# Product of the q and k weights in the middle of projection 1, on projection 2's weight buffer, with ScalarE forming the weights' high parts

## The chip, the cores and the metric

One core of one Trainium2 chip. The metric is the device time of the whole kernel in microseconds (us), lower is better; kernels are compared by the median of their runs. The engines are TensorE (PE, with its weight loads as PEld), VectorE (DVE), ScalarE (ACT), GpSimd (POOL) and SP, which only issues DMAs here.

## The reference

A decoder layer on 1024 tokens of width 1024 in float32. With h the modulated norm of the input:

```
proj = h @ w_in                      # xa, va, oa, za, gates, qa, ka, vat, zb, ga, gb
xc   = silu(causal_conv(xa))         # per channel, width 4
q_m  = xc_head @ w_q[head];  k_m = xc_head @ w_k[head] / 16
h_m  = mlstm_chunkwise(q_m, k_m, v_m, i, f)       # 4 heads of 256
o_a  = merged dilated window attention            # 3 groups x 4 heads of 128
y    = sigmoid(ga) * (h_m' @ w_out_mlstm) + sigmoid(gb) * (o_a' @ w_out_attn)
out  = rms_norm(x + gate * (y @ w_out))
```

What matters here is `w_in`, which is multiplied chunk by chunk, and that the kernel never forms q_m and k_m both: scores are xc (w_q w_k^T) xc^T, so each head multiplies its q weights with its k weights once (256x256 from 256 terms).

## The kernel before

Every float32 product with weights is done in three passes (`three_pass`, L477): each operand is split into a high part, the value rounded to the matmul's input type, and a low part, the rest; high x high, high x low and low x high are added up in the bank.

The stages are setup, mixing (`mix`, L484), merging (`merge`, L1174), finishing. The mixing stage runs over 4 heads. For each head there are 19 weight chunks of 128x1024, numbered q in the order of use: 18 projections (n = 0 to 17) and one chunk with the q and k weights of the head, at place FOLD = 3 (L37). Projections 0 and 1 make the inputs of the convolution; 2 to 5 are projections over tokens (values and output gate; matmuls of 256 columns, `project_tokens`, L612), the others (`project`, L598) have matmuls of 512. Each is done in two halves of the tokens, h = 0 and 1, of 24 matmuls of 512 or 48 of 256.

The path of a chunk: SP loads it into `wraw[q % 2]` (`load`, L528) once the split of chunk q - 2 is done. GpSimd splits it (`gpsimd`, L578): the high part into `whi[q % 2]`, as an addition of zero, and then the low part into `wlo[q % 2]`. It starts when chunk q - 2 has been multiplied (the semaphore `proj`, which every half counts up by one, and the weight product by two) and when the load has landed. TensorE waits for `w_split`, which the low part counts up. So while TensorE works on one buffer, the other is loaded with parts.

TensorE runs its program in order (`tensor`, L592). In its loop over n (L748) `fold_weights` (L638) stands ahead of projection 3: 12 matmuls of 256 columns into bank A1. Between the halves of projection 5 it uses this product (`head_q`); from projection 6 on the mLSTM's chunks, and from 9 on attention, lie between the halves.

ScalarE (`scalar`, L775) copies each half's bank out (`keep`), which frees the bank for the same half of the next projection (semaphores `kept`). Behind `keep` of either half come its other duties: sigmoids of the convolution, splitting xc and the weight product (`xc_high`, `fold_high`), exponentials. In projection 17 it first waits (L911) for the softmax statistics of all groups: they go out to DRAM by SP (`save_stats`), come back by another layout (`turn_stats`, which stands behind the load issued in projection 17), and VectorE works on them (`weigh_groups`, L1087) before ScalarE's exponential. Only then ScalarE copies out the second half of projection 17.

VectorE runs the convolution beside projections 0 and 1, then `fold_low` and `merge_groups` of the head before. In head 0 it first ends the setup: a chain of operations on the 4x1024 gate rows (L433 to L447), whose results SP writes to DRAM (L265 to L267), waits for, and reads back (L560, L561) before its first load of the stage, which is projection 3's weights (L564). The weights of the first four chunks were loaded in the setup.

Of the kernel before, what the change touches and what calls it, by code (L numbers as in the profile page):

```python
# [20 lines left out]
P = 128  # L21
D = 1024
S = 1024
KT = D // P
# [9 lines left out]
KSCALE = DH ** -0.5  # L34
MAIN = 18
CHUNKS = MAIN + 1
FOLD = 3  # L37
MERGE0 = HEADS * CHUNKS

XA, VA, OA, QKV, ZA, ZB = 0, 2, 4, 6, 15, 17  # L40
# [1 line left out]
AHEAD = 4  # L42
NADA = 5
PI = float(np.pi)


class Steps:
# [20 lines left out]
def stored(ap, g, lo=0, n=S):  # L68

    d = DIL[g]  # L70
    return ap.rearrange("p (r u) -> p r u", r=d)[:, :, lo // d:(lo + n) // d]


def build(nc, a, out):
# [409 lines left out]
def mix(nc, a, sem, ps, T):  # L484
# [12 lines left out]
    cb = [qm[:, 0, :], qm[:, 1, :], vt[:].rearrange("p c q -> p (c q)")]  # L497
    tn = [turn[:, b, 3:3 + S] for b in range(2)]

    summed, o_sig = sem("summed"), sem("o_sig")  # L500
    fold_split = sem("fold_split")
    xc_high_done, xc_split, zb_done = sem("xc_high_done"), sem("xc_split"), T["zb_done"]
    hp_in, ready, gr_in, hc_turned, hc_done = (T["hp_in"], *(sem(n) for n in ("mix_ready", "gr_in", "hc_turned", "hc_done")))
# [73 lines left out]

    def gpsimd(pool):  # L578
        pool.sem_inc(w_split, 2)
        for q in range(MERGE0):  # L580
            raw, hi, lo = wraw[:, q % 2, :], whi[:, q % 2, :], wlo[:, q % 2, :]
            pool.wait_ge(proj, 2 * q + 2)
            pool.wait_ge(w_in[q % 2], (q // 2 + 1) * 16)
            nc.gpsimd.tensor_tensor(hi, raw, zero[:].broadcast_to([P, D]), ALU.add).then_inc(pool_s, 1)  # L584
            pool.wait_ge(pool_s, q + 1)
            nc.gpsimd.tensor_tensor(lo, raw, hi.bitcast(F32), ALU.subtract).then_inc(w_split, 1)  # L586

    def blocks(g, tile):
# [3 lines left out]
    def tensor(pe):  # L592
        t_ = nc.tensor
        for i in range(0, HEADS):
# [3 lines left out]
            def project(n, h):  # L598
                q = chunk(n)
                pe.wait_ge(w_split, q + 3)  # L600
                pe.wait_ge(kept[h], i * MAIN + n + 1)
                for k in range(KT):
                    mm = three_pass(t_, ps[:, h, :], whi[:, q % 2, k * P:(k + 1) * P], wlo[:, q % 2, k * P:(k + 1) * P],
                                    h_hi[:, k, h * HALF:(h + 1) * HALF], h_lo[:, k, h * HALF:(h + 1) * HALF],
                                    k == 0, k == KT - 1)
                mm.then_inc(proj, 1)
# [5 lines left out]
            def project_tokens(n, h):  # L612

                q = chunk(n)
                pe.wait_ge(w_split, q + 3)
                if n == VA and h == 0:
                    pe.wait_ge(out_used, i * 4 + 4)
                    pe.wait_ge(masked, i * 24 + 1)
                if n == OA and h == 0:
                    pe.wait_ge(kept[0], i * MAIN + XA + 3)  # L620
                    pe.wait_ge(kept[1], i * MAIN + XA + 3)
                if n == OA and h == 1:
                    pe.wait_ge(p_kept, i * 12 + 1)
                    pe.wait_ge(pv_kept, i * 12 + 1)
                    pe.wait_ge(hc_done, 2)
                    pe.wait_ge(fold_split, i * 2 + 2)
                if n in (VA + 1, OA + 1):
                    pe.wait_ge(kept[h], i * MAIN + n + 1)
                for c in range(4 * h, 4 * h + 4):
                    to = ps[:, TOKEN_BANKS[n // 2 * 2][c // 2], (c % 2) * DH:(c % 2 + 1) * DH]  # L630
                    for j in range(KT // 2):
                        k = n % 2 * (KT // 2) + j
                        w = slice(j * DH, (j + 1) * DH)
                        mm = three_pass(t_, to, h_hi[:, k, c * P:(c + 1) * P], h_lo[:, k, c * P:(c + 1) * P],
                                        whi[:, q % 2, w], wlo[:, q % 2, w], j == 0, j == KT // 2 - 1)
                mm.then_inc(proj, 1)

            def fold_weights():  # L638

                q = i * CHUNKS + FOLD  # L640
                pe.wait_ge(w_split, q + 3)
                pe.wait_ge(p_kept, i * 12 + 1)
                pe.wait_ge(pv_kept, i * 12 + 1)
                w_hi, w_lo = (w[:, q % 2, :].rearrange("p (j e d) -> p j e d", j=2, e=2) for w in (whi, wlo))
                for d in range(2):
                    for e in range(2):
                        cols = slice(d * P, (d + 1) * P)
                        mm = three_pass(t_, A1[:, d * DH:(d + 1) * DH], w_hi[:, 0, e, cols], w_lo[:, 0, e, cols],
                                        w_hi[:, 1, e, :], w_lo[:, 1, e, :], e == 0, e == 1)
                mm.then_inc(proj, 2)  # L650
# [96 lines left out]

            for n in range(MAIN):  # L748
                c, g = n - 7, (n - 9) // 3
                if n == FOLD:  # L750
                    fold_weights()
                product = project_tokens if VA <= n < QKV else project
                product(n, 0)
                if n == 5:
                    head_q()
                if n == 6:
                    scores_and_keys(0)
                if 0 <= c < NCH:
                    numerator(c)
                if n >= 9:  # L760
                    attend(g, 2 * (n - 9 - 3 * g))
                product(n, 1)
                if n == 2 and i == 0:
                    pe.wait_ge(gr_in, 16)
                    pe.wait_ge(pv_kept, 1)
                    t_.transpose(A2[:, 0:P], gr[:], ident[:]).then_inc(hc_turned, 1)
                if 0 <= c < NCH - 1:
                    state_update(c)
                    scores_and_keys(c + 1)
                if n == 15:  # L770
                    turn_output()
                if n >= 9:
                    attend(g, 2 * (n - 9 - 3 * g) + 1)

    def scalar(act):  # L775
# [2 lines left out]
        act.sem_inc(pv_kept, 1)  # L778

        for i in range(0, HEADS):  # L780
            def chunk(n):
                return i * CHUNKS + n + (n >= FOLD)

            def keep(n, h):

                act.wait_ge(proj, 2 * chunk(n) + h + 5)
                src, fn = ps[:, h, :], ACT.Copy
                tok = slice(h * HALF, (h + 1) * HALF)
                if n < 2:
# [24 lines left out]
                    dst = szb[:, tok]  # L814
                A(dst, src, fn).then_inc(kept[h], 1)  # L815

            def o_sigmoid(h):
                act.wait_ge(summed, i * 4 + h + 3)
                part = og[:, 4 * h:4 * h + 4, :]
                A(part, part, ACT.Sigmoid).then_inc(o_sig, 1)  # L820
# [16 lines left out]
                A(xc_hi[:, q, :], xc[:, q, :], ACT.Copy).then_inc(xc_high_done, 1)  # L837

            def fold_high():
                act.wait_ge(proj, 2 * (i * CHUNKS + FOLD) + 6)  # L840
                A(fold[:, 0].rearrange("p d e -> p (d e)"), A1, ACT.Copy, scale=KSCALE).then_inc(fold_split, 1)

            def head_keep():
# [52 lines left out]
            for n in range(MAIN):  # L896
                c, g = n - 7, (n - 9) // 3
                keep(n, 0)
                if n == 1:
                    conv_sigmoid(0)  # L900
                if n == 2:
                    xc_high(0)
                    conv_sigmoid(1)
                if n == 5:
                    head_keep()
                if 0 <= c < NCH:
                    inter(c)
                if n >= 9:
                    attend(g, 2 * (n - 9 - 3 * g))
                if n == ZB:  # L910
                    act.wait_ge(ct_arg, i + 1)  # L911
                    A(cw[:, 1], cw[:, 1], ACT.Exp).then_inc(ct_exp, 1)
                if n == QKV:
                    o_sigmoid(0)
                keep(n, 1)
                if n == QKV:
                    o_sigmoid(1)
                if n == 2:
                    xc_high(1)
                    fold_high()  # L920
                    if i == 0:
                        head_decays()
                if n == 5:
                    intra_weights()
                if n == 14:
                    rstd()
                if n >= ZA:
                    z_sigmoid(n)
                if n >= 9:
                    attend(g, 2 * (n - 9 - 3 * g) + 1)  # L930
# [243 lines left out]
def merge(nc, a, sem, ps, T):  # L1174
# [9 lines left out]
    Q0 = MERGE0  # L1184
# [36 lines left out]
    def gpsimd(pool):  # L1221
        def split(l, at):

            n = width(l)
            pool.wait_ge(proj, 2 * at + (PROJ0 - 2))
            pool.wait_ge(w_in[l % 2], 8 * at + (8 * (Q0 - l % 2) + 16))
            nc.gpsimd.tensor_tensor(whi[:, l % 2, 0:n], raw[:, l % 2, 0:n], zero[:].broadcast_to([P, n]), ALU.add).then_inc(pool_s, 1)  # L1227
            pool.wait_ge(pool_s, at + (Q0 + 1))
            nc.gpsimd.tensor_tensor(wlo[:, l % 2, 0:n], raw[:, l % 2, 0:n], whi[:, l % 2, 0:n].bitcast(F32), ALU.subtract)\
              .then_inc(w_split, 1)  # L1230

        for l in range(4):
            split(l, l)
        for t in range(0, KT // 2 - 1):
            for j in range(8):
                split(4 + j, t * 8 + (4 + j))
        for l in range(28, 32):
            split(l, l)
# [332 lines left out]
```

## Time and profile before

| | |
|---|---|
| three runs | 1516.88, 1517.12 and 1518.81 us, median 1517.12 |
| profiled execution | 1520.18 us, its span 1518.3 |
| TensorE busy | 1437.2 us, 95% of the span |
| VectorE busy | 809.8 us, 53% |
| ScalarE busy | 430.3 us, 28% |
| GpSimd busy | 553.7 us, 36% |
| mixing stage | about 75 to 1114 us, a head some 259 us |

The span is that of the profiled execution's instructions, on one core. A matmul's end is modelled, so a busy TensorE is one that has work, not one at its peak. The granted clock is the share of 2.4 GHz that TensorE was given.

### The profile page before, as it was taken

How to read it: one execution, taken by the hardware profiler on the slowest of the kernel's cores; microseconds unless marked ns; L12 is line 12 of the kernel's file. 1: busy time of each engine (PE TensorE's matmuls, PEld its weight loads, DVE VectorE, ACT ScalarE, POOL GpSimd, SP SyncE). 2: the span in 40 equal slices, each digit the busy share in tenths (PEclk: the TensorE clock that was granted, in tenths of full speed). 3: DMA queues.
4: the chain of work that ended last, by engine and by line, in shares of the span. 5: the costliest groups of instructions: out<-in, count | busy, mean ns of one | idle time of the engine just before them, and what ended most of it. 6: DMA issues, size and time to landing. Idle time of an engine off the chain costs nothing.

```text
span 1518.3 us, 18422 instructions
## 1 busy us (share of the span) xinstructions
PE 1437.2 (95%) x7481; PEld 1237.1 (81%) x7481; DVE 809.8 (53%) x1251; ACT 430.3 (28%) x803; POOL 553.7 (36%) x269
## 2 busy tenths in 40 slices
PE   2498999998999999899999989999999999999997
PEld 2388888887988888898888889888888888888885
DVE  7995455747555564835656482565557111111565
ACT  7432322333132234222223323222333000001243
POOL 2635322334432223533223353323244444444551
PEclk9799999999999999999999999999999999999999
DMA  7622011123210112311101322111145111114433
GB/s 281 220 70 73 31 42 29 29 43 115 80 43 28 42 29 46 113 67 42 43 28 32 101 68 67 42 29 30 41 142 199 63 63 63 63 62 153 160 129 111
DMA packets 49659, 118.04 MB, mean 78 GB/s; under 512 B 20512, under 2 KB 20640, under 8 KB 49572
## 3 DMA queue, kind: packets, MB, share of 16 engines
q1 hardware_dynamic: 45480, 103.75, 21.3%
q10 hardware_dynamic: 2976, 9.06, 1.7%
q0 software_dynamic: 1120, 4.06, 0.8%
q8 instruction: 60, 0.98, 0.3%
q14 instruction: 23, 0.19, 0.0%
HBM read 101.42 MB, written 15.43 MB: 77 GB/s over the span
## 4 chain that ended last, share of the span: by engine, by line
PE 90%; DVE 6%; POOL 1%; issue 1%; DMA 1%; ACT 0%; ACTq 0%; SPq 0%; DVEq 0%; POOLq 0%
PE banks L479 26%; PE banks L481 26%; PE banks L480 26%; DVE s_crow L371 2%; PE banks L735 2%; PE banks L725 2%; PE banks L686 2%; PE banks L692 2%; PE banks L744 1%; PE banks L673 1%; PE banks L684 1%; POOL wlo L586 1%; PE banks L713 1%; POOL whi L584 1%; DVE s_acc_g L425 1%
## 5 line engine op out<-in xcount | busy, mean ns | idle before, releaser
L479 PE MATMUL banks<-h_hi,whi 128*128 128x512 f32 x1152 | 458.5, 398 | 0.0
L481 PE MATMUL banks<-h_hi,wlo 128*128 128x512 f32 x1152 | 449.8, 390 | 0.0
L480 PE MATMUL banks<-h_lo,whi 128*128 128x512 f32 x1152 | 448.8, 390 | 0.0
L584 POOL TENSOR_TENSOR whi<-wraw,zero 128x1024 fp32r<-128x1024 f32 x76 | 154.3, 2031 | 671.2 <-PE banks L481 659.8
L481 PEld LDWEIGHTS banks<-h_hi,wlo 128*128 128x128 f32 x1152 | 216.2, 188 | 45.9
L480 PEld LDWEIGHTS banks<-h_lo,whi 128*128 128x128 f32 x1152 | 216.6, 188 | 42.8
L479 PEld LDWEIGHTS banks<-h_hi,whi 128*128 128x128 f32 x1152 | 216.5, 188 | 42.5 <-issue 0.3
L586 POOL TENSOR_TENSOR wlo<-wraw,whi 128x1024 fp32r<-128x1024 f32 x76 | 204.5, 2691 | 6.0
L479 PE MATMUL banks<-whi,h_hi 128*128 128x256 f32 x512 | 149.2, 291 | 20.4 <-POOL wlo L586 20.4
L480 PE MATMUL banks<-wlo,h_hi 128*128 128x256 f32 x512 | 148.5, 290 | 0.0
L481 PE MATMUL banks<-whi,h_lo 128*128 128x256 f32 x512 | 148.3, 290 | 0.0
L1227 POOL TENSOR_TENSOR whi<-wraw,zero 128x1024 fp32r<-128x1024 f32 (+1 forms) x32 | 55.1, 1721 | 184.3 <-PE banks L481 179.6
L479 PEld LDWEIGHTS banks<-whi,h_hi 128*128 128x128 f32 x512 | 102.2, 200 | 21.5 <-POOL wlo L586 21.2
L1337 DVE TENSOR_TENSOR num<-qa,banks 128x512 f32<-128x512 f32 x16 | 11.0, 688 | 184.6 <-PE banks L481 175.6
L480 PEld LDWEIGHTS banks<-wlo,h_hi 128*128 128x128 f32 x512 | 102.1, 199 | 0.3
L481 PEld LDWEIGHTS banks<-whi,h_lo 128*128 128x128 f32 x512 | 102.0, 199 | 0.0
L815 ACT ACTIVATE turn<-banks 128x512 f32<-128x512 f32 (+1 forms) x56 | 40.5, 722 | 216.9 <-PE banks L481 216.9
L1296 ACT ACTIVATE qa<-banks 128x512 f32<-128x512 f32 x32 | 19.1, 597 | 233.6 <-PE banks L481 233.6
L1027 DVE SCALAR_TENSOR_TENSOR cst<-cst,dec,banks 128x257 f32<-128x257 f32 x56 | 24.5, 480 | 104.5 <-PE banks L692 104.5
L479 PE MATMUL banks<-b_hi,whi 128*128 128x512 f32 x192 | 74.7, 389 | 0.0
L480 PE MATMUL banks<-b_lo,whi 128*128 128x512 f32 x192 | 74.7, 389 | 0.0
L481 PE MATMUL banks<-b_hi,wlo 128*128 128x512 f32 x192 | 74.7, 389 | 0.0
(251 smaller groups left out, 2236.0 us busy)
## 6 DMA issues: line engine op xcount, KB each, us to landing
wraw<-in_w_all SPq DMA_DIRECT2D x100, 512.0 KB, 3.5
s_wada<-in_w_ada_cols SPq DMA_DIRECT2D x16, 512.0 KB, 5.2
raw_lo<-in_x SPq DMA_DIRECT2D x8, 512.0 KB, 9.8
s_wada<-in_w_ada_gate SPq DMA_DIRECT2D x8, 512.0 KB, 3.6
qm<-group_weights SPq DMA_DIRECT2D x8, 512.0 KB, 6.7
mlstm_branch<-xc SPq DMA_DIRECT2D x8, 512.0 KB, 9.1
b_raw<-mlstm_branch SPq DMA_DIRECT2D x8, 512.0 KB, 6.9
merged<-num ACTq DMA_DIRECT2D x8, 512.0 KB, 2.6
```

The lines of the kernel that those rows point to most:

```text
L371: v.tensor_tensor_reduce(crow[:, 2, :], wada[:, n % NADA, :], crow[:, 1, :], 1.0, bc[:, (j - 1) * KT + k:(j - 1) * KT + k + 1], ALU.mult, ...
L479: t_.matmul(out, w_hi, x_hi, start=first, stop=False)
L480: t_.matmul(out, w_hi, x_lo, start=False, stop=False)
L481: return t_.matmul(out, w_lo, x_hi, start=False, stop=last)
L584: nc.gpsimd.tensor_tensor(hi, raw, zero[:].broadcast_to([P, D]), ALU.add).then_inc(pool_s, 1)
L586: nc.gpsimd.tensor_tensor(lo, raw, hi.bitcast(F32), ALU.subtract).then_inc(w_split, 1)
L686: mm = t_.matmul(M2[:, 0:DH + 1], qm[:, d, c * P:(c + 1) * P], cst[:, d, :], start=(d == 0), stop=(d == 1))
L692: mm = t_.matmul((M1, M2)[d][:, 0:DH + 1], kw[:, c % 2, d * P:(d + 1) * P], v1[:, c, 0:DH + 1], start=True, stop=True)
L725: mm = t_.matmul(A0[:, u * 2 * P:u * 2 * P + b * P], qa[:, g % 2, 0, t * P:(t + 1) * P], qa[:, g % 2, 1, (t + 1 - b) * P:(t + 1) * P], sta ...
L735: mm = t_.matmul(A2[:, u * P:(u + 1) * P], vt[:, t + 1 - b + j, :], pT[:, u, j, :], start=(j == 0), stop=(j == b - 1))
L815: A(dst, src, fn).then_inc(kept[h], 1)
L1227: nc.gpsimd.tensor_tensor(whi[:, l % 2, 0:n], raw[:, l % 2, 0:n], zero[:].broadcast_to([P, n]), ALU.add).then_inc(pool_s, 1)
```

## The change

`FOLD` becomes 2: the chunk with the q and k weights stands third of the 19, and its product is formed between the halves of projection 1. Projection 2 follows in the same buffer: `slot` gives a chunk's buffer in `whi` and `wlo`, while `wraw` goes on alternating by q. `product_done` and `fold_done` give the values of `proj` that the new order has. ScalarE forms the high parts of all chunks but the first two (`weights_high`): that of projection 2 after the copy of projection 1's first half, that of the product's weights after projection 0's second copy, the others after the second copy of each projection; the last two are for the merging stage. GpSimd keeps the low parts, and waits for the high ones (`w_high`). The transposition of the gate rows on TensorE and ScalarE's use of it move from projection 2 to the middle of projection 3, in head 0.

```
-FOLD = 3
+FOLD = 2
+def slot(q):
+    n = q % CHUNKS
+    return n % 2 if n <= FOLD else (n - 1) % 2
+def product_done(i, n, h):
+    return 4 + 2 * (i * CHUNKS + n + (n >= FOLD)) + h + (3 if (n, h) == (FOLD - 1, 1) else 1)
+def fold_done(i):
+    return product_done(i, FOLD - 1, 0) + 2
...
     def gpsimd(pool):
         pool.sem_inc(w_split, 2)
-        for q in range(MERGE0):
-            raw, hi, lo = wraw[:, q % 2, :], whi[:, q % 2, :], wlo[:, q % 2, :]
-            pool.wait_ge(proj, 2 * q + 2)
-            pool.wait_ge(w_in[q % 2], (q // 2 + 1) * 16)
-            nc.gpsimd.tensor_tensor(hi, raw, zero[:].broadcast_to([P, D]), ALU.add).then_inc(pool_s, 1)
-            pool.wait_ge(pool_s, q + 1)
+        for q in range(MERGE0 + 2):
+            raw, hi, lo = wraw[:, q % 2, :], whi[:, slot(q), :], wlo[:, slot(q), :]
+            if q < 2:
+                pool.wait_ge(w_in[q], 16)
+                nc.gpsimd.tensor_tensor(hi, raw, zero[:].broadcast_to([P, D]), ALU.add).then_inc(pool_s, 1)
+                pool.wait_ge(pool_s, q + 1)
+            else:
+                pool.wait_ge(w_high, q - 1)
             nc.gpsimd.tensor_tensor(lo, raw, hi.bitcast(F32), ALU.subtract).then_inc(w_split, 1)
...
             for n in range(MAIN):              # TensorE
-                if n == FOLD:
-                    fold_weights()
                 product(n, 0)
+                if n == FOLD - 1:
+                    fold_weights()
+                if n == 3 and i == 0:
+                    pe.wait_ge(gr_in, 16)
+                    pe.wait_ge(pv_kept, 1)
+                    t_.transpose(A2[:, 0:P], gr[:], ident[:]).then_inc(hc_turned, 1)
...
                 product(n, 1)
-                if n == 2 and i == 0:
-                    pe.wait_ge(gr_in, 16)
-                    pe.wait_ge(pv_kept, 1)
-                    t_.transpose(A2[:, 0:P], gr[:], ident[:]).then_inc(hc_turned, 1)
...
+            def weights_high(q, free):         # ScalarE
+                act.wait_ge(proj, free)
+                act.wait_ge(w_in[q % 2], (q // 2 + 1) * 16)
+                A(whi[:, slot(q), :], wraw[:, q % 2, :], ACT.Copy).then_inc(w_high, 1)
...
                 keep(n, 0)
                 if n == 1:
+                    weights_high(i * CHUNKS + FOLD + 1, fold_done(i))
                     conv_sigmoid(0)
...
+                if n == 3 and i == 0:
+                    head_decays()
...
                 keep(n, 1)
+                weights_high(i * CHUNKS + (FOLD if n == 0 else n + 3), product_done(i, n, 1))
...
                     fold_high()
-                    if i == 0:
-                        head_decays()
...
-        for l in range(4):                     # merging stage, GpSimd
+        for l in range(2, 4):
             split(l, l)
```

## Rows read from the trace of the kernel before

**Rows 1.** TensorE's waits in total: engine, line, released by: us, times, longest us
```profile
PE banks L479 <- POOL wlo L586: 20.4, 4, 7.9
```

**Rows 2.** Timeline of TensorE: start us, us, operation, [idle before, released by]
```profile
110.19 0.33 PE L766 MATMUL banks<-ident,gr 128*128 128x128 f32 x1 [1.45 <-DMA gr<-gate_rows]
...
119.90 0.58 PE L479 MATMUL banks<-whi,h_hi 128*128 128x256 f32 x1 [7.94 <-POOL wlo L586]
...
373.54 0.28 PE L481 MATMUL banks<-whi,wlo 128*128 128x256 f32 x1
...
377.95 0.58 PE L479 MATMUL banks<-whi,h_hi 128*128 128x256 f32 x1 [4.13 <-POOL wlo L586]
```

**Rows 3.** Windows: us, busy us (instructions) by engine, PEclk (granted clock), DMA share, GB/s
```profile
110.20:111.60 1.40, 1.40 (x12) 1.40 (x13) 0.28 (x1) 1.38 (x2) 0.00 (x0) 1.00 0.50 60
...
380.00:382.00 2.00, 2.00 (x12) 2.00 (x11) 2.00 (x1) 0.00 (x0) 1.92 (x2) 0.50 0.31 125
...
384.00:386.00 2.00, 2.00 (x19) 2.00 (x18) 2.00 (x1) 0.00 (x0) 0.88 (x1) 1.00 0.17 20
```

**Rows 4.** Timeline of GpSimd, first halves of splits, four heads
```profile
86.43 3.41 POOL L584 TENSOR_TENSOR whi<-wraw,zero 128x1024 fp32r<-128x1024 f32 x1 [19.92 <-PE banks L481]
...
113.97 2.59 POOL L584 TENSOR_TENSOR whi<-wraw,zero 128x1024 fp32r<-128x1024 f32 x1 [11.39 <-DMA wraw<-in_w_all]
...
133.48 1.89 POOL L584 TENSOR_TENSOR whi<-wraw,zero 128x1024 fp32r<-128x1024 f32 x1 [7.45 <-PE banks L481]
...
360.95 1.89 POOL L584 TENSOR_TENSOR whi<-wraw,zero 128x1024 fp32r<-128x1024 f32 x1 [6.18 <-PE banks L481]
...
372.47 2.15 POOL L584 TENSOR_TENSOR whi<-wraw,zero 128x1024 fp32r<-128x1024 f32 x1 [6.81 <-PE banks L481]
...
392.13 2.90 POOL L584 TENSOR_TENSOR whi<-wraw,zero 128x1024 fp32r<-128x1024 f32 x1 [7.25 <-PE banks L481]
...
631.21 2.15 POOL L584 TENSOR_TENSOR whi<-wraw,zero 128x1024 fp32r<-128x1024 f32 x1 [6.81 <-PE banks L481]
...
651.17 2.58 POOL L584 TENSOR_TENSOR whi<-wraw,zero 128x1024 fp32r<-128x1024 f32 x1 [7.56 <-PE banks L481]
...
890.14 2.15 POOL L584 TENSOR_TENSOR whi<-wraw,zero 128x1024 fp32r<-128x1024 f32 x1 [6.81 <-PE banks L481]
...
908.81 2.76 POOL L584 TENSOR_TENSOR whi<-wraw,zero 128x1024 fp32r<-128x1024 f32 x1 [6.23 <-PE banks L481]
```

**Rows 5.** Timeline of ScalarE, bank copies at the start of head 1
```profile
343.31 0.58 ACT L815 ACTIVATE szb<-banks 128x512 f32<-128x512 f32 x1
...
350.03 0.60 ACT L815 ACTIVATE turn<-banks 128x512 f32<-128x512 f32 x1 [2.96 <-PE banks L481]
...
355.47 0.60 ACT L815 ACTIVATE turn<-banks 128x512 f32<-128x512 f32 x1 [4.84 <-PE banks L481]
```

**Rows 6.** GpSimd's low parts of weights: duration ns min/median/max, starts
```profile
L586 POOL TENSOR_TENSOR wlo<-wraw,whi x76: 2367/2403/4255, 58.2 to 1088.6; 128x1024 fp32r<-128x1024 f32 x76
```

**Rows 7.** ScalarE's instructions by form: busy us, mean ns | idle us
```profile
L837 ACT ACTIVATE xc_hi<-xc 128x1024 fp32r<-128x1024 f32 x8 | 8.4, 1054 | 0.9 <-DVE xc L965 0.9
```

**Rows 8.** Landing of the weight loads of the mixing stage (L531)
```profile
DMA to landing us min/median/max: 3.3/3.5/7.1
```

**Rows 9.** Timeline of VectorE, gate rows of head 0, statistics of head 1
```profile
92.02 3.23 DVE L440 TENSOR_TENSOR s_xnT<-s_xnT 4x1024 f32<-4x1024 f32 x1
...
95.48 1.21 DVE L442 TENSOR_TENSOR s_xnT<-s_xnT,s_mprev 4x1024 f32<-4x1024 f32 x1
...
340.87 2.27 DVE L1094 TENSOR_TENSOR cw<-ct,cw 128x24 f32<-128x24 f32 x1
...
343.43 0.18 DVE L1096 TENSOR_TENSOR cw<-cw,ct 128x24 f32<-128x24 f32 x1 [0.29 <-ACT cw L912]
```

**Rows 10.** Timeline of SP's queue, before head 0's projection 3
```profile
103.69 0.33 SPq L265 DMA_DIRECT2D gate_rows<-s_xnT  x1
...
109.31 0.89 SPq L531 DMA_DIRECT2D wraw<-in_w_all  x2
```

More of the change, by code:

```diff
@@ L498, in mix @@
     tn = [turn[:, b, 3:3 + S] for b in range(2)]
-    summed, o_sig = sem("summed"), sem("o_sig")
+    summed, o_sig, w_high = sem("summed"), sem("o_sig"), sem("w_high")
     fold_split = sem("fold_split")
@@ L602, in project @@
                 for k in range(KT):
-                    mm = three_pass(t_, ps[:, h, :], whi[:, q % 2, k * P:(k + 1) * P], wlo[:, q % 2, k * P:(k + 1) * P],
+                    mm = three_pass(t_, ps[:, h, :], whi[:, n % 2, k * P:(k + 1) * P], wlo[:, n % 2, k * P:(k + 1) * P],
                                     h_hi[:, k, h * HALF:(h + 1) * HALF], h_lo[:, k, h * HALF:(h + 1) * HALF],
@@ L634, in project_tokens @@
                         mm = three_pass(t_, to, h_hi[:, k, c * P:(c + 1) * P], h_lo[:, k, c * P:(c + 1) * P],
-                                        whi[:, q % 2, w], wlo[:, q % 2, w], j == 0, j == KT // 2 - 1)
+                                        whi[:, n % 2, w], wlo[:, n % 2, w], j == 0, j == KT // 2 - 1)
                 mm.then_inc(proj, 1)
@@ L643, in fold_weights @@
                 pe.wait_ge(pv_kept, i * 12 + 1)
-                w_hi, w_lo = (w[:, q % 2, :].rearrange("p (j e d) -> p j e d", j=2, e=2) for w in (whi, wlo))
+                w_hi, w_lo = (w[:, slot(q), :].rearrange("p (j e d) -> p j e d", j=2, e=2) for w in (whi, wlo))
                 for d in range(2):
@@ L780, in scalar @@
         for i in range(0, HEADS):
-            def chunk(n):
-                return i * CHUNKS + n + (n >= FOLD)
             def keep(n, h):
-                act.wait_ge(proj, 2 * chunk(n) + h + 5)
+                act.wait_ge(proj, product_done(i, n, h))
                 src, fn = ps[:, h, :], ACT.Copy
@@ L839, in fold_high @@
             def fold_high():
-                act.wait_ge(proj, 2 * (i * CHUNKS + FOLD) + 6)
+                act.wait_ge(proj, fold_done(i))
                 A(fold[:, 0].rearrange("p d e -> p (d e)"), A1, ACT.Copy, scale=KSCALE).then_inc(fold_split, 1)
@@ L1227, in split @@
             nc.gpsimd.tensor_tensor(whi[:, l % 2, 0:n], raw[:, l % 2, 0:n], zero[:].broadcast_to([P, n]), ALU.add).then_inc(pool_s, 1)
-            pool.wait_ge(pool_s, at + (Q0 + 1))
+            pool.wait_ge(pool_s, at + 1)
             nc.gpsimd.tensor_tensor(wlo[:, l % 2, 0:n], raw[:, l % 2, 0:n], whi[:, l % 2, 0:n].bitcast(F32), ALU.subtract)\
               .then_inc(w_split, 1)
-        for l in range(4):
+        for l in range(2, 4):
             split(l, l)
```

## The prediction

> **What bounds the kernel now.** I read the waits of TensorE first, then its timeline where that wait ends, then the granted clock there, then GpSimd's timeline as a ruler, and last the queues that feed it. In this stage TensorE waits for one engine only: 20.4 us in 4 waits for GpSimd's low parts, one a head [rows 1]. In head 1 the last matmul of the weight product starts at 373.54 and the next projection's first at 377.95, after 4.13 us of idleness [rows 2]. The reader is to see what follows it as well: the granted clock is 0.50 (1.2 GHz) at 380 to 382 us, with 12 matmuls in the window, and back at 1.00 (2.4 GHz) at 384 to 386, with 19 [rows 3]. In head 0 TensorE idles 1.45 us for the transposition of the gate rows, and right behind it the clock is 1.00 [rows 2, 3]; then it idles 7.94 us [rows 2]. So a wait of 4 us brings a half-rate stretch, one of 1.45 us did not.
>
> GpSimd's first half of a split waits only for TensorE to finish two chunks earlier, so its starts date the chunk ends [rows 4]. A projection over tokens takes 372.47 - 360.95 = 11.52 us for 96 matmuls of 256 columns, 0.12 each; halves of the others take 5.44 (355.47 - 350.03, the ends seen by ScalarE's copies, [rows 5]). The weight product has 12 matmuls of 256 columns: 12 x 0.12 = 1.44. Undisturbed, product and projection 3 would take 1.44 + 11.52 = 12.96 us from the end of projection 2. They take 392.13 - 372.47 = 19.66, 651.17 - 631.21 = 19.96 and 908.81 - 890.14 = 18.67 us in heads 1 to 3 [rows 4]: 6.70, 7.00 and 5.71 lost, 19.4 together. Of each some 4.2 are idleness, the rest half rate. In head 0 projection 2 ends at 110.19 - 1.45 = 108.7 and projection 3 at 133.48 [rows 2, 4], 24.8 for 12.96: 11.8 lost. All four: 31.2.
>
> Why: a buffer holds a projection's weights for 11 us, time for a split of 4.3 (1.89 [rows 4] + 2.40 [rows 6]), but the product's weights only for 1.44 us. The chunk behind it is split after projection 2 ends.
>
> **The change, part by part, heads 1 to 3** (times of head 1).
>
> *The product's weights* go into buffer 0, which projection 0 leaves at 350.03. ScalarE's copy of the bank, 0.60 [rows 5], then the high part: the same form, 128x1024 to the same type, took 1.054 [rows 7], so it ends near 351.75. GpSimd's low part had a median of 2.40 us, a maximum of 4.25 [rows 6]: ready at 354.2, latest 356.1. TensorE wants it after the first half of projection 1, at 355.47 [rows 5]. VectorE starts its convolution at about this time; behind one such instruction (1.2) the low part is there at 355.3. I take no wait; the bound is 0.7 a head.
>
> *Projection 2's weights* follow into the same buffer. Product done at 355.47 + 1.44 = 356.9; ScalarE is then done with its copy (356.07), high part to 358.0, low part to 360.5, latest 362.3. TensorE comes at 356.9 + 5.44 = 362.4: nothing. Their load is issued after the split of projection 1's weights and takes 3.5 us (median; 7.1 at most) [rows 8], early enough.
>
> *Projection 3's weights* have the other buffer from 362.4, ready near 367.6, wanted at 362.4 + 11.52 = 373.9. That is the wait that goes, and with it the half rate. What is late next is only the two links above.
>
> *76 high parts on ScalarE* are 80 us of work added, on an engine busy 28% of the span. They stand right behind the copy that frees the bank, so TensorE's bank waits are not delayed. What is queued behind them moves by 1.05: exponentials, sigmoids, and at the head's end the exponentials whose maxima and sums go out to DRAM. That chain comes back as VectorE's small operations; until they are done ScalarE stands in front of the last bank copy of the head, at 343.31, done at 343.9 [rows 5]. TensorE needs this bank half a projection before 350.03, at 344.6. Only 0.7 us are spare, and 1.05 is added. Against it: VectorE's subtraction of 24 elements took 2.27 us at 340.87, a like one 0.18 at 343.43 [rows 9], and it ended as GpSimd's split did; that split now comes after ScalarE's copy. So 2.1 go and 1.05 come. I take nothing, bounds +0.4 and 0 at each of four head ends.
> The Trainium skill (GPSIMD Engine Reference, section Specifications) says that GpSimd shares its SBUF interfaces with VectorE and contends with instructions that have two SBUF inputs. The 2.27 against 0.18 agrees with it.
>
> *GpSimd* loses one of two instructions a chunk. It was not on the path but for the four waits.
>
> **Head 0** is another matter. Its weights for projection 3 are not split earlier, because they come late: GpSimd waited 11.39 us for their load [rows 4]. SP issued it at 109.31, after VectorE's gate rows had gone out at 103.69 and come back [rows 10]; it landed at 113.97, 4.66 later. The change helps only by freeing VectorE: of its row operations four are stretched, such as 3.23 us at 92.02 against 1.21 at 95.48 [rows 9], 7.3 us together, behind four GpSimd instructions (two splits). Two remain, and the first falls on the scan. Following the queue I get rows out at 101.2, 2.5 earlier; bounds 0 and 7.3. Then 5.62 to the load's issue, 4.66 to landing: 111.5; high part 112.5; low part, behind a convolution instruction of 1.3 at worst, 115.0 to 116.3, taken 115.6. Projection 3 starts at 115.7 instead of 119.90: 4.2 gained. TensorE gets to its end of projection 2 at 86.4 + 10.88 + 1.44 + 11.52 = 110.3, plus up to 0.9 if the product's low part lands late (88.1 + 4.25 = 92.4 against 91.8), so a wait of about 5 stays, and with it the half rate (133.48 - 119.90 - 11.52 = 2.06 lost, unchanged). The transposition of the gate rows moves to projection 3 and no longer waits; its 1.45 is inside the 4.2. Bounds for this head: 0.5 gained (load as late as now, 113.97 + 1.05 + 4.25) and 11 (all gone).
>
> The Trainium skill (TensorE: Matmul & The Clock Gate, section Why this matters for your kernels) warns that idle gaps between bursts of matmuls bring the low clock back. [...]
>
> **Sum.** 19.4 + 4.2 = 23.6 us. The profiled execution took 1520.18 (span 1518.3, 1.9 around it): 1496.6. It stands 3.1 above the median of the runs, 1517.12, so that median becomes 1493.5. Behind the mixing stage nothing is touched but the first two splits of the merging stage, hidden under a whole projection, so the gain is kept.
>
> **Rivals.**
> 1. *A new short wait at both places of each head.* ScalarE to GpSimd is now a chain of 4 to 6 us against half a projection, 5.44. For it: 4.25 has occurred, and the copy stands first. Against: it came behind a scan that only head 0 has. Price at 1.2 us a place, the length of one VectorE instruction more than counted: 3 x 2 x 1.2 = 7.2, so 1501. Chance 0.15.
> 2. *Head 0 loses its wait too*, if the rows get out 7.3 earlier: 31.2 - 1 = 30, so 1487. For: all four stretched operations lie beside a split. Against: two splits stay. Chance 0.10.
> 3. *The idleness goes, the half rate stays*, if gaps under 1 us at the new places are enough: (19.4 - 3 x 4.2) / 3 = 2.3 a head, 3 x 2.3 = 6.9 back, 1500. The 1.45 us gap speaks against it. Chance 0.06.
> 4. *Slower: the ring through ScalarE at the head's end.* The next head's first split waits for ScalarE; SP's load of its product weights waits for that split; the read-back of the statistics stands behind this load in SP's queue; ScalarE waits for the statistics before its last bank copy, the next high part behind it. One us of lateness beyond the 0.7 spare is then one of TensorE, at four head ends, and from some 2 us on half rate is added (2.3). It decides when the statistics come over 4.3 us later than now: 4 x (3.6 + 2.3) eats the 23.6. At 6 us late: 4 x (5.3 + 2.3) - 23.6 = +6.8, 1524. For: so little is spare today, and 1.05 comes. Against: each other piece has slack, and VectorE's 2.1 us go. Chance 0.07, of which 0.03 within the uncertainty.
> 5. *It does not do what it says*: the splits at the product don't shorten, since the low part waits for VectorE each time. With 4.25 each the wait is 0.7 a head, inside the forecast.
>
> **How the numbers follow.** Forecast 0.62, rivals 0.15, 0.10, 0.06, 0.07. The likeliest gives 1493.5, its own range 1490 to 1497. Two in ten left out: 1486 (rival 2) to 1502 (rivals 1 and 3). This kernel's measurement can tell some 0.2% (3 us) from nothing: slower only by rival 4, 0.04; within 0.03 by its milder form and 0.01 for what I don't see; faster 0.92.
>
> **What would show it.** Right: TensorE's waits for the low parts in heads 1 to 3 below 0.7 us, granted clock 1.00 through projection 3, a distance of 12.96 from the end of projection 2 less the product, and one wait of about 5 us in head 0 with the load of projection 3's weights landing at 111 to 112. Wrong: a wait ahead of the product or of projection 2, bank waits at the head starts (ScalarE's last copy of head 0 ending less than half a projection before projection 0 does), or a load in head 0 no earlier than 113.9.

## The result and the profile after

The kernel after takes 1499.45 us (median of 4 runs, 1498.71 to 1499.88), the one before 1517.03 beside it: 17.6 us less, ratio 0.9881, 95% interval 0.9864 to 0.9898. Run again in a later comparison it took 1498.89 (0.9870, 0.9854 to 0.9887). The forecast was 1493.5 us, 23.6 less. The direction and the outer range (1486 to 1502) held; the forecast's own range, 1490 to 1497, did not, and the size is off by 6 us.

The page of the kernel after (first line, TensorE's busy time, its granted clock in 40 slices):

```profile
span 1498.0 us, 18420 instructions
...
PE 1429.0 (95%) x7481; PEld 1229.0 (82%) x7481; DVE 759.6 (51%) x1251; ACT 501.3 (33%) x879; POOL 392.9 (26%) x193
...
PEclk9799999999999999999999999999999999999999
```

TensorE's waits in the kernel after (engine and line, released by: us in total, times, longest):

```profile
PE banks L477 <- DVE raw_lo L425: 27.0, 1, 27.0
PE banks L495 <- DVE h_lo L399: 12.9, 1, 12.9
PE banks L495 <- POOL h_lo L316: 10.6, 5, 6.3
PE banks L495 <- issue: 7.1, 1, 7.1
```

The 20.4 us behind GpSimd's low parts [rows 1] are gone; all but the last of these rows belong to the setup. What is new is the last row: 7.1 us once, on "issue", a wait for which the profile shows no releaser.

Head 1, TensorE's timeline at the new place of the product:

```profile
354.21 0.39 PE L497 MATMUL banks<-h_hi,wlo 128*128 128x512 f32 x1
354.44 0.28 PE L495 MATMUL banks<-whi 128*128 128x256 f32 x1
...
355.75 0.28 PE L497 MATMUL banks<-whi,wlo 128*128 128x256 f32 x1
355.87 0.40 PE L495 MATMUL banks<-h_hi,whi 128*128 128x512 f32 x1
...
361.34 0.28 PE L495 MATMUL banks<-whi,h_hi 128*128 128x256 f32 x1
```

The reader is to see that TensorE goes from the first half of projection 1 (512 columns) to the product's first matmul, and from the product's last to the second half, without a wait, where [rows 2] had 4.13 us. The last row is the first matmul of projection 2; it has no wait either. ScalarE and GpSimd of the same stretch, which the two new links run through (L830 is the bank copy, L836 the high part, L604 the low part):

```profile
341.20 0.58 ACT L830 ACTIVATE szb<-banks 128x512 f32<-128x512 f32 x1
...
349.20 0.60 ACT L830 ACTIVATE turn<-banks 128x512 f32<-128x512 f32 x1 [3.33 <-PE banks L497]
349.69 1.05 ACT L836 ACTIVATE whi<-wraw 128x1024 fp32r<-128x1024 f32 x1
354.64 0.60 ACT L830 ACTIVATE turn<-banks 128x512 f32<-128x512 f32 x1 [3.89 <-PE banks L497]
356.07 1.06 ACT L836 ACTIVATE whi<-wraw 128x1024 fp32r<-128x1024 f32 x1 [0.83 <-PE banks L497]
...
361.54 0.60 ACT L830 ACTIVATE turn<-banks 128x512 f32<-128x512 f32 x1 [3.45 <-PE banks L497]
...
373.05 1.03 ACT L830 ACTIVATE v<-banks 128x1024 f32<-128x1024 f32 x1 [2.84 <-PE banks L497]
```

```profile
350.82 2.39 POOL L604 TENSOR_TENSOR wlo<-wraw,whi 128x1024 fp32r<-128x1024 f32 x1 [5.61 <-ACT whi L836]
357.21 2.40 POOL L604 TENSOR_TENSOR wlo<-wraw,whi 128x1024 fp32r<-128x1024 f32 x1 [4.00 <-ACT whi L836]
363.16 3.46 POOL L604 TENSOR_TENSOR wlo<-wraw,whi 128x1024 fp32r<-128x1024 f32 x1 [3.55 <-ACT whi L836]
```

The product's weights: projection 0 ends at 349.20, the bank is copied, the high part starts at 349.69, the low part is done at 353.21; TensorE comes at 354.44. Projection 2's weights: the product is done, the high part starts at 356.07, the low part is done at 359.61; TensorE comes at 361.34. So 1.2 and 1.7 us are spare, and the same in heads 2 and 3. Windows of the kernel after (us, busy us of the engines, PEclk, DMA share, GB/s), the first behind the wait in head 0, the others over projection 3 of head 1:

```profile
100.10:102.00 1.90, 1.90 (x9) 1.90 (x10) 1.65 (x3) 0.00 (x0) 0.00 (x0) 0.50 0.08 9
373.00:379.00 6.00, 6.00 (x53) 6.00 (x52) 2.99 (x2) 3.60 (x5) 2.41 (x1) 1.00 0.10 20
379.00:385.00 6.00, 6.00 (x53) 6.00 (x52) 5.90 (x5) 1.27 (x2) 0.00 (x0) 1.00 0.18 70
```

At 380 to 382 us the clock was 0.50 before [rows 3]; now it is 1.00 throughout. The only half-rate stretch of the mixing stage is the one in head 0 (0.50 at 100 to 102).

Where the time went is best measured head by head, from ScalarE's copy of projection 0's second half to the same copy of the next head (after the last head, of the merging stage's first chunk, at 1104.99):

```profile
1104.99 0.60 ACT L1319 ACTIVATE qa<-banks 128x512 f32<-128x512 f32 x1 [3.80 <-PE banks L497]
```

| us | start of head 0 | head 0 | head 1 | head 2 | head 3 | from there to the end |
|---|---|---|---|---|---|---|
| before | 86.4 | 263.6 | 258.7 | 258.9 | 257.7 | 392.9 |
| before, second profile | 88.0 | 260.7 | 259.1 | 257.6 | 258.4 | 393.0 |
| after | 87.6 | 261.6 | 251.9 | 251.9 | 251.9 | 393.0 |

Heads 1 to 3 give 19.5 us against the profile of before (775.3 to 755.8), where 19.4 were forecast. Head 0 gives 2.0 where 4.2 were forecast, and against the second profile of before it loses 0.9. The rest is the setup, 1.2 us later than in the profile of before. It is no effect of the change: over the eleven profiles of this case the end of projection 0 in head 0 lies anywhere from 86.2 to 88.0 us, at 86.4 and 88.0 in the two of the kernel before, at 87.6 and 86.3 in the two of the kernel after.

### The profile page after: what moved, and what is told of

It reads as the page before. It is cut to its first block, busy times and chain, and to the rows that moved or that the text cites. A ratio compares the mean times of both kernels' runs of the same rounds, so it can differ in the third digit from the quotient of the medians.

```text
span 1498.0 us, 18420 instructions
## 1 busy us (share of the span) xinstructions
PE 1429.0 (95%) x7481; PEld 1229.0 (82%) x7481; DVE 759.6 (51%) x1251; ACT 501.3 (33%) x879; POOL 392.9 (26%) x193
## 4 chain that ended last, share of the span: by engine, by line
PE 94%; DVE 4%; issue 1%; DMA 0%; ACT 0%; POOL 0%; ACTq 0%; DVEq 0%
PE banks L495 27%; PE banks L497 27%; PE banks L496 27%; DVE s_crow L387 2%; PE banks L753 2%; PE banks L743 2%; PE banks L704 2%; PE banks L710 2%; PE banks L762 1%; PE banks L691 1%; PE banks L702 1%; PE banks L731 1%; PE banks L720 1%; DVE s_angle L412 0%; PE banks L693 0%
## 5 line engine op out<-in xcount | busy, mean ns | idle before, releaser
L604 POOL TENSOR_TENSOR wlo<-wraw,whi 128x1024 fp32r<-128x1024 f32 x78 | 201.1, 2578 | 838.9 <-ACT whi L836 838.8
L495 PE MATMUL banks<-whi,h_hi 128*128 128x256 f32 x512 | 144.9, 283 | 0.0
L497 PE MATMUL banks<-whi,h_lo 128*128 128x256 f32 x512 | 144.9, 283 | 0.0
L496 PE MATMUL banks<-wlo,h_hi 128*128 128x256 f32 x512 | 144.9, 283 | 0.0
L830 ACT ACTIVATE turn<-banks 128x512 f32<-128x512 f32 (+1 forms) x56 | 40.5, 723 | 192.8 <-PE banks L497 192.8
L496 PEld LDWEIGHTS banks<-wlo,h_hi 128*128 128x128 f32 x512 | 98.2, 192 | 0.3
L495 PEld LDWEIGHTS banks<-whi,h_hi 128*128 128x128 f32 x512 | 98.2, 192 | 0.3
L497 PEld LDWEIGHTS banks<-whi,h_lo 128*128 128x128 f32 x512 | 98.2, 192 | 0.0
L1250 POOL TENSOR_TENSOR whi<-wraw,zero 128x1024 fp32r<-128x1024 f32 (+1 forms) x30 | 50.6, 1688 | 162.9 <-PE banks L497 162.9
L836 ACT ACTIVATE whi<-wraw 128x1024 fp32r<-128x1024 f32 x76 | 79.8, 1051 | 11.9 <-PE banks L497 11.9
```

The source lines that it names most:

```text
L495: t_.matmul(out, w_hi, x_hi, start=first, stop=False)
L496: t_.matmul(out, w_hi, x_lo, start=False, stop=False)
L497: return t_.matmul(out, w_lo, x_hi, start=False, stop=last)
L836: A(whi[:, slot(q), :], wraw[:, q % 2, :], ACT.Copy).then_inc(w_high, 1)
```

## The experiments

Every kernel was timed beside the kernel before.

### The kernel before once more

> The kernel before, unchanged, for a second profile. The profiled execution of before took 1520.18 us against a median of 1517.03, 3.1 more; that of the kernel after 0.4 more than its median. Theory: the profiled execution of before was an uncommon one (setup or half-rate stretches longer than usual), so the traces overstate the gain (20.3 us by profiled executions, 17.6 by medians). Then this one takes 1517 to 1518 in its profile too, with the difference in the setup or in the half-rate stretches of the heads. Rival: profiling itself costs this kernel 3 us, then 1520 again. Timed: ratio 1.000 within 0.001.

Measured: 1517.93 us (ratio 1.0001, 0.9993 to 1.0010), its profiled execution 1518.58, span 1516.8. TensorE's wait ahead of projection 3 in head 0, in this profile:

```profile
117.89 0.58 PE L479 MATMUL banks<-whi,h_hi 128*128 128x256 f32 x1 [6.01 <-POOL wlo L586]
```

The rival falls: the profiled execution lies 0.65 us over its median and not 3. Of the theory the difference in head 0 is right, but not the setup, which is 1.6 us longer here, and 1518.58 is just over the 1517 to 1518 expected. The wait is 6.01 us, where [rows 2] has 7.94, and there is no wait for the gate rows. The half-rate stretches of heads 1 to 3 are as many as before. SP writes the gate rows 14.1 us after the end of projection 0 (102.09 - 87.99), where it took 17.3 (103.69 - 86.39). So the profile on which the prediction was built had a head 0 that was 2.9 us longer than this one, by VectorE's chain on the gate rows. Which comes more often isn't settled by two profiles. The medians of the runs lie by the shorter; but in a later comparison 2 of 15 runs of this kernel took 1520.2 and 1520.6 us, so such a time comes without the profiler too. By this profile the recoverable loss was 28 us and not 31.

### Bank A1 released by ScalarE

```
         act.sem_inc(pv_kept, 1)
+        act.sem_inc(p_kept, 1)
...
-        for s, k in ((num_kept, 1), (normed, 1), (p_kept, 1)):
+        for s, k in ((num_kept, 1), (normed, 1)):
             dve.sem_inc(s, k)
```

> The kernel after; the first release of bank A1 (p_kept counted up once) is given by ScalarE at the start of its mixing program and no longer by VectorE, which gets there only after the gate rows (99.8 us). Theory: the 7.1 us wait ahead of the weight product in head 0 is this release; it goes, the product starts at about 93.4, right behind the low part. Then projection 3's load is the next limit: it lands about 111 and TensorE waits some 4 us ahead of projection 3, with a half-rate stretch. Time 1499.5 - 3 = 1496.5 us. Rival: the wait is for something else (the low part, bank A2): no change, 1499.5.

Measured: 1495.67 us (0.9856, 0.9842 to 0.9869), 3.2 to 3.8 less than the kernel after. The wait ahead of the product is gone; in its place is this one ahead of projection 3, and a window behind it:

```profile
114.75 0.39 PE L495 MATMUL banks<-whi,h_hi 128*128 128x256 f32 x1 [3.80 <-POOL wlo L604]
```

```profile
114.80:117.00 2.20, 2.20 (x12) 2.20 (x13) 1.08 (x2) 1.19 (x2) 0.00 (x0) 0.62 0.59 145
```

The wait of 3.80 us and the clock of 0.62 over the window behind it (0.50 from 116 to 118) are what the prediction had for head 0 (5 us and a half-rate stretch). The theory holds, the rival falls.

### The early load alone

```
         sp.dma_start(acc_d, acc_g[:]).then_inc(setup_out, 16)
+        T["first_weights"](sp, range(AHEAD, AHEAD + 1))
         sp.wait_ge(rows_ready, 4)
...
-                load(i * CHUNKS + p + AHEAD)
+                if i + p:
+                    load(i * CHUNKS + p + AHEAD)
```

> The kernel after; the load of projection 3's weights in head 0 is issued by SP before it waits for the gate rows. Theory: in the kernel after this load isn't the limit any more, because TensorE has lost 7.1 us earlier: same time, 1499.5 within 1 us, and still 7.1 us of wait ahead of the product. Rival (the load was what bound head 0, as predicted): 4 us faster, 1495.5.

Measured: 1498.85 us (0.9874, 0.9861 to 0.9888), no difference from the kernel after, as expected. SP's queue, and TensorE's wait:

```profile
92.55 0.33 SPq L155 DMA_DIRECT2D wraw<-in_w_all  x1
98.24 0.32 SPq L282 DMA_DIRECT2D gate_rows<-s_xnT  x1
```

```profile
PE banks L496 <- issue: 6.6, 1, 6.6
```

The load goes out at 92.55, 12.1 us earlier than at 104.69 in the kernel after (shown below), and nothing comes of it. In the kernel after the load had stopped being the limit of head 0.

### Both

The two edits above together.

> Both: bank A1 released by ScalarE and projection 3's weights of head 0 loaded ahead of the gate rows. Theory: no wait is left in head 0 but at most 0.5 us ahead of the product, and no half-rate stretch in the mixing stage: 7.1 + 2.3 = 9.4 us less, 1490 us. Rival: a third limit stands close behind (VectorE's convolution, or the clock): 1494 or more.

Measured: 1491.27 us (0.9827, 0.9813 to 0.9840). There is no half-rate stretch left in the mixing stage, and head 0 takes 253.7 us. One wait remains, and ScalarE's timeline shows why:

```profile
111.90 0.39 PE L496 MATMUL banks<-whi,h_hi 128*128 128x256 f32 x1 [1.19 <-POOL wlo L606]
```

```profile
106.35 1.06 ACT L857 ACTIVATE sg<-cv 128x1024 f32<-128x1024 f32 x1 [10.21 <-DVE cv L983]
107.31 0.58 ACT L833 ACTIVATE turn<-banks 128x512 f32<-128x512 f32 x1
107.79 1.05 ACT L839 ACTIVATE whi<-wraw 128x1024 fp32r<-128x1024 f32 x1
```

ScalarE stands at the first convolution's sigmoid (L857) until VectorE has done the convolution, which it starts only behind the gate rows. The copy of projection 1's second half and the high part of projection 3's weights (L839) stand behind it, 8 us after TensorE was done. 1491.3 is between theory and rival, near the theory: a third limit exists and costs 1.2 us.

### Both, and the sigmoid last

```
                     weights_high(i * CHUNKS + FOLD + 1, fold_done(i))
-                    conv_sigmoid(0)
+                    if i:
+                        conv_sigmoid(0)
...
                 weights_high(i * CHUNKS + (FOLD if n == 0 else n + 3), product_done(i, n, 1))
+                if n == 1 and i == 0:
+                    conv_sigmoid(0)
```

> The kernel with bank A1 released by ScalarE and the early load, and in head 0 ScalarE's first convolution sigmoid put behind the second copy and the high part of projection 1. The trace of the kernel with the first two edits shows 1.2 us of wait ahead of projection 3 in head 0, with ScalarE standing at this sigmoid until 106.4 us, so that copy and high part come at 107.3 and 107.8 instead of 99. Theory (ScalarE's queue is the third limit): this wait goes, 1.2 us less than that kernel, 1490 us. Rival (VectorE's chain sets it through the convolution anyway): no change, 1491.3, or a new wait at projection 4.

Measured: 1490.89 us (0.9821, 0.9806 to 0.9835). Expected 1490; the 0.4 us to the kernel with both can't be told from nothing. The wait moved instead of going:

```profile
117.49 0.36 PE L496 MATMUL banks<-whi,h_hi 128*128 128x256 f32 x1 [1.17 <-ACT v L833]
```

The rival holds: it is now ahead of projection 3's second half, for the copy of projection 2, which stands behind the second convolution's sigmoid. VectorE's chain from the gate rows through two convolutions is the limit of head 0 from here on: ScalarE waits 3.85 us for the second convolution, until 115.38, and copies projection 2 only then. No run here shortens that chain. This is the fastest of the kernels, with the one before it level: 26 to 27 us less than before, 8 less than the kernel after.

### The order alone: GpSimd forms the high parts too

```
             else:
-                pool.wait_ge(w_high, q - 1)
+                pool.wait_ge(proj, ...)        # the product that frees slot(q)
+                pool.wait_ge(w_in[q % 2], (q // 2 + 1) * 16)
+                nc.gpsimd.tensor_tensor(hi, raw, zero[:].broadcast_to([P, D]), ALU.add).then_inc(pool_s, 1)
+                pool.wait_ge(pool_s, q + 1)
...
-                    weights_high(i * CHUNKS + FOLD + 1, fold_done(i))
...
-                weights_high(i * CHUNKS + (FOLD if n == 0 else n + 3), product_done(i, n, 1))
```

> The kernel after, but GpSimd forms the high parts too: the order and the buffers alone. From the end of projection 0 GpSimd needs 1.89 + 2.40 = 4.3 us for the product's weights, up to 1.3 more behind VectorE's convolution, against 5.44 of half a projection; the same from the product to projection 2. Theory (the new place of the product is the whole gain in heads 1 to 3): 1499.5 to 1502 us, waits of at most 0.5 us a place. Rival (ScalarE's part is needed): waits of 1 us and more at both places of each head, 1506 or more.

The last two lines are taken out of ScalarE's program. Measured: 1501.82 us (0.9889, 0.9876 to 0.9903). GpSimd's timeline at the product in head 1:

```profile
349.98 1.89 POOL L611 TENSOR_TENSOR whi<-wraw,zero 128x1024 fp32r<-128x1024 f32 x1 [7.13 <-PE banks L497]
351.95 2.72 POOL L613 TENSOR_TENSOR wlo<-wraw,whi 128x1024 fp32r<-128x1024 f32 x1
356.85 1.97 POOL L611 TENSOR_TENSOR whi<-wraw,zero 128x1024 fp32r<-128x1024 f32 x1 [2.18 <-PE banks L497]
358.91 3.27 POOL L613 TENSOR_TENSOR wlo<-wraw,whi 128x1024 fp32r<-128x1024 f32 x1
```

The low parts end at 354.7 and 362.2. TensorE's first matmul of the product starts at 355.18 and that of projection 2 at 362.23, so nothing is spare at the second place; by the pace of the kernel after (12.14 us from the copy of projection 0, here at 349.94) it would have started at 362.08. Heads 1 to 3 take 252.2 to 252.4 us. So the order and the shared buffer give 18.5 of the 19.5 us in these heads; ScalarE's part gives 1.0 there. In head 0 the kernel after is 1.3 us shorter, and TensorE's wait ahead of the product is 7.1 us instead of 8.0; but that wait is for VectorE's chain (7.6 in the kernel after's second profile), so how much of this is ScalarE's part stays open. The theory holds.

### ScalarE's part alone

The product stays at its old place; `weights_high(q)` follows the second copy of each projection and, for the chunk behind the product, `fold_high`.

> The kernel before, but ScalarE forms the high parts; the product stays ahead of projection 3. From the end of projection 2: bank copy 1.03, high part 1.05, low part 2.4 to 3.2, 4.5 to 5.3 us against the 5.4 of before. Theory: the wait ahead of projection 3 stays at 3 to 4 us a head, with its half-rate stretch: 1514 to 1517.5 us. Rival: half of the gain comes from the faster splits: 1508 or less.

Measured: 1516.69 us (0.9987, 0.9978 to 0.9996). TensorE's waits for the low parts:

```profile
PE banks L479 <- POOL wlo L588: 18.0, 5, 7.7
```

18.0 us, against 20.4 [rows 1] and 18.4 in the second profile of before. In heads 1 to 3 the wait is 3.05 us each instead of 4.13, with a stretch at 0.50 behind each of the three, and these heads take 771.5 us, 3.8 less than before. In head 0 there are two waits, 1.13 us ahead of the product and 7.72 ahead of projection 3, and the head takes 263.6 us, as in the first profile of before and 2.9 more than in the second. So a faster split helps little where the buffer is free only 1.44 us early. The theory holds.

### Each high part formed twice

```
                 A(whi[:, slot(q), :], wraw[:, q % 2, :], ACT.Copy).then_inc(w_high, 1)
+                act.wait_ge(w_high, 2 * q - 3)
+                A(whi[:, slot(q), :], wraw[:, q % 2, :], ACT.Copy).then_inc(w_high, 1)
...
-                pool.wait_ge(w_high, q - 1)
+                pool.wait_ge(w_high, 2 * q - 2)
```

> The kernel after, with each high part formed twice by ScalarE (1.05 us more in each split and on ScalarE). In heads 1 to 3 of the kernel after the product's low part ends about 1.4 us ahead of TensorE, projection 2's about 1.9 us, the last bank copy of a head 2 us. Theory: all three hold 1.05 us more, so 1499.5 to 1501 us. Rival (the chain over ScalarE is at its limit): a wait at two places a head, with half-rate stretches, 1506 or more.

Measured: 1502.65 us (0.9896, 0.9883 to 0.9910), 3.2 more than the kernel after, and neither theory nor rival. The two links hold, as the theory said; what gives way is another place. TensorE's waits for ScalarE in the mixing stage:

```profile
PE banks L762 <- ACT sm L916: 2.1, 4, 0.5
...
PE banks L495 <- ACT szb L830: 0.2, 1, 0.2
```

Line 762 is the transposition of attention's exponentials, in projection 17; these stand on ScalarE behind projection 16's copy, high part and sigmoid. TensorE waits 0.5 us for them in each head. The same exponentials end at 331.5 in the kernel after and TensorE wants them at 332.0, so the kernel after has 0.5 us to spare here, less than at the two links. Heads 1 to 3 take 759.2 us, 3.4 more than in the kernel after; three of these four waits and the 0.2 us for the last bank copy explain some 1.8 of it, and the rest stays open; there is no half-rate stretch in them.

### The kernel after once more

> The kernel after, unchanged, beside the others of this call: 1499.5 us within 1, a wait of 6.5 to 7.5 us ahead of head 0's product, no half-rate stretch in heads 1 to 3.

Measured: 1498.89 us. The wait ahead of the product was 7.6 us, just over the range given; heads 1 to 3 have no half-rate stretch.

## Why the prediction was right, and by how much it was off

**The stall and the half rate behind it, heads 1 to 3.** Right in mechanism and size: 19.4 forecast, 19.5 measured. That idleness and half rate go together is seen in both directions: every wait of 3.05 us and more in the mixing stage of these kernels has a stretch at 0.50 behind it, those of 0.5 to 1.5 have none. Rival 3 falls. It falls by the trace and not by the time: 1499.45 us lies at the prices of rivals 3 and 1, 1500 and 1501, and is inside the outer range because that range made room for them.

**The two new links.** Forecast without a wait, and none came; spare are 1.2 and 1.7 us. I had the low part of the product's weights at 354.2 to 355.3, against TensorE at 355.47; it came 1.2 ahead. Rival 1 falls.

**The end of the head.** VectorE's subtraction went from 2.27 us [rows 9] to 0.18, as forecast:

```profile
340.86 0.18 DVE L1117 TENSOR_TENSOR cw<-ct,cw 128x24 f32<-128x24 f32 x1
```

In the second profile of before this subtraction took 0.18 too, but another operation of the same chain, of 8 columns, took 2.36 instead of 0.17 (128x8); the chain was stretched once either way, and in the kernel after it is not at any of the four head ends. ScalarE's last copy now starts at 341.20, where it was 343.31 [rows 5]; against the end of the next projection 0 that is 1.3 us earlier, so 2.0 us are spare where it was 0.7. The ring of rival 4 did not close, but it isn't far at every head: at the end of head 1 the statistics come later and only 0.6 us are spare (copy done at 595.1, bank needed at 595.7). The other point that has become tight was not among my rivals: the exponentials of projection 17, with 0.5 us spare.

**Head 0: the step that failed.** The prediction put the product at 91.8 to 92.4 us, "if the product's low part lands late", and looked for its wait only there. But `fold_weights` waits for `p_kept` too, and the first count of `p_kept` is given by VectorE at the start of its mixing program, behind the whole chain on the gate rows. Before, the product stood ahead of projection 3, and the count was there at 104.4 us, 4 us ahead of it. TensorE, and VectorE's start on the mixing program, in the kernel after:

```profile
100.07 0.55 PE L495 MATMUL banks<-whi 128*128 128x256 f32 x1 [7.09 <-issue]
```

```profile
91.20 3.23 DVE L456 TENSOR_TENSOR s_xnT<-s_xnT 4x1024 f32<-4x1024 f32 x1
...
99.80 0.06 DVE L959 MEMSET turn<- 128x6 f32 x1
```

The second VectorE row is the instruction behind which the count is given; TensorE starts 0.2 us after its end. That this is the cause is shown by the kernel with the release moved, where the wait is gone. This replaced the predicted wait of 5 us ahead of projection 3 by one of 7.1 ahead of the product. The chain of the gate rows came out shorter than forecast: SP writes the rows at 99.07, 11.5 us after the end of projection 0, where it was 17.3 and the forecast had 14.8 (101.2 - 86.4), and issues the load at 104.69 where it was 109.31 [rows 10]:

```profile
99.07 0.33 SPq L281 DMA_DIRECT2D gate_rows<-s_xnT  x1
...
104.69 0.42 SPq L547 DMA_DIRECT2D wraw<-in_w_all  x1
```

Part of that is owed to the new wait, which keeps the second split (104.14) behind the chain. With the release moved to ScalarE the chain has two stretched operations again, as forecast, and the rows go out after 13.2 us (100.14 - 86.95). In the kernel after none of it counts, since TensorE is late on its own. ScalarE's copies of projection 0 and of projection 3, second halves, in head 0 of the second profile of before and of the kernel after:

```profile
87.99 0.60 ACT L815 ACTIVATE turn<-banks 128x512 f32<-128x512 f32 x1 [3.40 <-PE banks L481]
...
132.02 1.03 ACT L815 ACTIVATE turn<-banks 128x1024 f32<-128x1024 f32 x1 [2.54 <-PE banks L481]
```

```profile
87.58 0.60 ACT L830 ACTIVATE turn<-banks 128x512 f32<-128x512 f32 x1 [3.41 <-PE banks L497]
...
132.70 1.03 ACT L830 ACTIVATE turn<-banks 128x1024 f32<-128x1024 f32 x1 [3.13 <-PE banks L497]
```

44.0 us before, 45.1 after. With the release moved, head 0 takes 257.8 us, 3.8 less than in the kernel after; the forecast stood at 263.6 - 4.2 = 259.4. So the missed wait costs 3.8 us, and 1.6 come back, as much as the gate rows go out earlier than forecast (13.2 us after the end of projection 0, not 14.8). By spans of profiled executions the sum would then have held within 1.1 us: 1518.3 - 23.6 = 1494.7, against 1493.6 measured; by medians the kernel with the release moved takes 1495.67, 2.2 over the forecast.

**The baseline.** The remaining 2.7 us of the 6 are the profile of before: it ran 3.1 us over its median, and I carried this through to the median as a constant. The profile of the kernel after lies 0.4 over its own. By profiled executions the gain is 20.3 us, by medians 17.6. Where in the kernel these 2.7 us lie isn't shown: the second profile of before has head 0 shorter by 2.9 and the setup longer by 1.6.

So of the 6 us, 2.2 are head 0 (3.8 for the missed wait less 1.6), 1.2 the later setup in the profile of after, and 2.7 the profile of before. Only the first is a fault of mechanism. This is by the profile that the prediction had.

## What to carry to other kernels

When a step is moved earlier in a program, read every wait it carries, and for each ask who gives its first count and when: a count that was free at the old place can be the last one at the new. A short product between long ones starves the buffer behind it; put it in the middle of a long one and let it share the buffer of the one that follows, and the split has half a projection. Before a gain is worked out from a profile that lies above its median, profile the kernel twice: what differs between the two is not there to be gained.

## What was not expected of the hardware

A VectorE operation with two inputs in SBUF runs at its bare time, or, when one of GpSimd's splits is under way, it ends only with or behind GpSimd's instruction: 0.18 us or 2.27 for 24 elements, 1.21 or 3.23 for 4x1024. The 2.27 us one [rows 9] ended at 343.14, GpSimd's low part at 343.10. The same step of the gate rows in the first profile of before, then in the second:

```profile
97.31 1.93 POOL L584 TENSOR_TENSOR whi<-wraw,zero 128x1024 fp32r<-128x1024 f32 x1 [3.14 <-PE banks L481]
...
97.41 2.90 DVE L445 TENSOR_TENSOR s_xnT<-s_xnT 4x1024 f32<-4x1024 f32 x1
```

```profile
98.91 2.08 POOL L584 TENSOR_TENSOR whi<-wraw,zero 128x1024 fp32r<-128x1024 f32 x1 [4.12 <-PE banks L481]
...
98.02 1.21 DVE L445 TENSOR_TENSOR s_xnT<-s_xnT 4x1024 f32<-4x1024 f32 x1
```

In the first VectorE comes 0.1 us behind GpSimd and ends 1.07 us after it, in the second it comes 0.9 us ahead and takes 1.21. From its first operation to SP's write the chain took 20.6 us in one profile of the same kernel and 18.4 in the next (83.11 to 103.69, 83.72 to 102.09); measured from the end of projection 0 it is 17.3 and 14.1, since in the second it also began 1.0 us earlier against TensorE. Two inputs are not the condition in every case. In the kernel with the sigmoid last a copy of 4x8 elements, which has one input and takes 0.16 us in the others, ended with GpSimd's low part (97.66 and 97.64):

```profile
95.41 2.25 DVE L460 COPY s_wlast<-s_xnT 4x8 f32<-4x8 f32 x1
```

A stretch like this is a draw, not a constant, and should be carried as a range.
